# Mixer A's attention with keys on partitions: scores of three heads in one matmul, maxima from an extra pass

## The reference

```python
def gqa_attention(q, k, v):                # 6 query heads, 2 key heads, head width 64
    ...
    scale = Dh ** -0.5
    def block(qblk):                       # 128 queries
        s = jnp.einsum('bqngd,bsnd->bngqs', qblk, k) * scale
        p = jax.nn.softmax(s, axis=-1)
        return jnp.einsum('bngqs,bsnd->bqngd', p, v)
    ...
# latent queries: keys are the 1024 latent keys and 128 cached context keys
out_a = gqa_attention(qa, jnp.concatenate([ka, ck_a], axis=1), jnp.concatenate([va, cv_a], axis=1))
# prompt queries: keys are the 128 prompt keys
out_a = gqa_attention(qa, ka, va)
```

## Time and profile before

| | us |
|---|---|
| median of 3 runs | 3603.79 (3602.97 to 3606.46) |
| the profiled execution, device time | 3604.08 |
| its span, first to last instruction | 3602.3 |
| tensor engine busy in the span | 3340.2 |
| mixer A's attention, layer 0 | 175.70 to 368.54 |
| mixer A's attention, layer 1 | 1952.90 to 2145.04 |

### The profile page before, as it was taken

One profiled execution on the slowest core, in us unless ns is written; L12 is line 12 of the kernel. 1 busy time (PEld: TensorE's weight loads), 2 busy tenths in 40 slices (PEclk: granted clock), 3 DMA queues, 4 the chain that ended last, 5 costly groups with the idle time before them and its releaser, 6 DMA issues. The chain is left out here.

```text
span 3602.3 us, 48329 instructions
## 1 busy us (share of the span) xinstructions
PE 3340.2 (93%) x18844; PEld 2783.5 (77%) x18844; DVE 1319.7 (37%) x2333; ACT 1496.2 (42%) x2904; POOL 1396.1 (39%) x836
## 2 busy tenths in 40 slices
PE   6799999987999999999986999998979999999998
PEld 4478666776789989989964876676857899999997
DVE  2656333156641131131127643333565311311212
ACT  3255333124554454454423543331335544444443
POOL 1400011015765565565523000000167555655654
PEclk8899999998999999999987999999989999999999
DMA  5000121146544444444400001110535444444443
GB/s 197 12 8 1 43 65 30 42 156 201 177 129 127 143 134 129 144 133 156 146 28 20 1 25 43 43 41 31 195 100 175 129 124 146 145 125 146 147 125 115
DMA packets 310450, 367.41 MB, mean 102 GB/s; under 512 B 20160, under 2 KB 252880, under 8 KB 310224
## 3 DMA queue, kind: packets, MB, share of 16 engines
q1 hardware_dynamic: 310080, 364.19, 31.8%
q10 hardware_dynamic: 144, 0.13, 0.0%
HBM read 343.97 MB, written 20.30 MB: 101 GB/s over the span
## 5 line engine op out<-in xcount | busy, mean ns | idle before, releaser
L2070 POOL TENSOR_TENSOR w_lo<-w_raw,w_hi 128x1024 fp32r<-128x1024 f32 x432 | 1054.1, 2441 | 720.4 <-ACT w_hi L1991 720.0
L1991 ACT CAST w_hi<-w_raw 128x1024 fp32r<-128x1024 f32 x432 | 453.6, 1050 | 916.0 <-PE ps L1941 547.6
L2100 DVE TENSOR_TENSOR u_lo<-mix,u_hi 128x384 fp32r<-128x384 f32 x192 | 266.6, 1388 | 1212.7 <-ACT u_hi L2002 1212.7
L1939 PE MATMUL ps<-h_hi,w_hi 128*128 128x384 f32 x1536 | 517.6, 337 | 2.8 <-ACT mix L1998 2.8
L1941 PE MATMUL ps<-h_hi,w_lo 128*128 128x384 f32 x1536 | 516.4, 336 | 0.0
L1940 PE MATMUL ps<-h_lo,w_hi 128*128 128x384 f32 x1536 | 515.3, 335 | 0.0
L1958 PE MATMUL ps<-w_hi,u_lo 128*128 128x512 f32 x1152 | 453.2, 393 | 0.0
L1957 PE MATMUL ps<-w_lo,u_hi 128*128 128x512 f32 x1152 | 453.0, 393 | 0.0
L1956 PE MATMUL ps<-w_hi,u_hi 128*128 128x512 f32 x1152 | 450.9, 391 | 0.0
L1939 PEld LDWEIGHTS ps<-h_hi,w_hi 128*128 128x128 f32 x1536 | 289.3, 188 | 10.0 <-issue 3.2
L1940 PEld LDWEIGHTS ps<-h_lo,w_hi 128*128 128x128 f32 x1536 | 289.1, 188 | 6.8
(11 more groups left out here) (267 smaller groups left out, 4988.0 us busy)
## 6 DMA issues: line engine op xcount, KB each, us to landing
w_raw<-in_w_ffn_up SPq DMA_DIRECT2D x192, 512.0 KB, 4.1
w_raw<-in_w_ffn_down SPq DMA_DIRECT2D x192, 512.0 KB, 3.3
ring<-in_w_ada SPq DMA_DIRECT2D x80, 512.0 KB, 5.7
out_y_sample<-x SPq DMA_DIRECT2D x32, 512.0 KB, 2.9
w_raw<-in_w_out SPq DMA_DIRECT2D x30, 512.0 KB, 3.5
x<-out_y_sample SPq DMA_DIRECT2D x24, 512.0 KB, 5.0
ring<-in_w_in SPq DMA_DIRECT2D x18, 512.0 KB, 5.4
w_raw<-in_w_out SPq DMA_DIRECT2D x36, 256.0 KB, 4.2
```

The source lines that it names most:

```text
L1939: pe.matmul(ps[:, 6, 0:CW], wh[:, k, :], hi[:, k, cc], start=(k == 0), stop=False)
L1991: act.copy(w_hi[:, i % 3, :], raw[:, i % 3, :]).then_inc(sem("piece_hi"), 1)
L2070: pool.tensor_tensor(w_lo[:, i % 3, :], raw[:, i % 3, :], w_hi[:, i % 3, :].bitcast(F32), ALU.subtract).then_inc(sem("piece_lo"), 1)
L2100: dve.tensor_tensor(u_lo[:, j % 2, m, :], square[:, i % 2, :], u_hi[:, j % 2, m, :].bitcast(F32), ALU.subtract).then_inc(sem("m_u_lo"), 1)
```

## The change

`attention()` is gone and `turned_attention()` takes its place, with a stream for POOL too. Keys lie on the partitions of the scores and queries along the columns, for the three query heads of one key head at once: `scores_turned(i, g)` puts 3 x 128 queries against one key slot. The result needs no transposes to be applied to the values. A row's maximum and sum now run across partitions, and are made in other ways:

- One extra pass, `scores(x)`: the scores in the old layout, with KH alone (512 + 512 + 128 columns), only for `maximum(x)` on DVE. All 54 units go through the same three banks, 0 to 2.
- POOL's `make_diag(i)` multiplies six identity matrices by a tile's six columns of maxima. `shift(i)` on the tensor engine sums them over the partitions (weights `select`, ones on one half), which lays the negated maxima along the columns, in bank 0. ACT's `copy_shift(i)` copies them to the free half of `q2`; POOL's `copy_high(i)` puts the high query part on the other.
- The low-key pass takes `q2` in place of Q: KL's free half now holds 1/64 in place of zero (`clear_low(pool, KL, 1.0 / HD)`), so 64 rows of 1/64 times the shift add it to each score in the same matmul.
- `exp(i, g)` needs no bias: 128x384 from one of three PSUM banks (3 to 5) to one of six slots of a ring in the free part of `mix`.
- Sums: DVE (`add`, "first", "pair", "more", "part") and POOL (`add`, "pair", "more") add the probabilities of the nine slots up into `total`; `denominator(i)` sums it over the partitions with a matmul of ones (fp32, 64-column halves), in bank 0; `output(i)` takes the reciprocal of 128x384 and multiplies the output of three heads by it.
- The tensor engine's order: steps of three key slots, three steps a latent tile, one for the prompt tile, which now comes last. Two units of the extra pass go into each step, up to two tiles ahead. The applies of a step follow a step later.
- `bank_free()` guards bank 0 to 2 before each `scores`, `shift` and `denominator`.

The diff, cut to its core:

```diff
-            def clear_low(pool, k_low):
+            def clear_low(pool, k_low, value=0.0):
...
-            def attention(tag, units, own, n_keys):
...
+            def turned_attention(Q, KH, KL, V, own):
+                TILES = list(range(LAT)) + [PROMPT]
+                SLOTS = [list(range(LAT)) + [CTX_SLOT]] * LAT + [[PROMPT]]
+                W = 3 * P
+                RING = 6
...
+                steps = [(i, c) for i in range(nt) for c in range((len(SLOTS[i]) + 2) // 3)]
+                units = [(i, j, m) for i in range(nt) for j in range(2) for m in range(3)]
...
+                def turned_scores(b):
+                    return ps[:, 3 + b % 3, 0:W]
+                def out_of(i):
+                    return ps[:, 6 + i % 2, 0:W]
+                def upto(s):
+                    return min(6 + min(3 * (s + 1), 2 * (s + 1) + 2), len(units))
+                def sum_ops(i, c):          # (DVE's adds, POOL's adds)
+                    g = list(chunk(i, c))
+                    if len(SLOTS[i]) == 1:
+                        return [("first", (g[0],))], []
+                    if c == 0:
+                        return [("pair", (g[0], g[1])), ("more", (g[2],))], []
+                    if c == 1:
+                        return [("more", (g[0],))], [("pair", (g[1], g[2]))]
+                    return [("more", (g[0],)), ("more", (g[1],)), ("part", ())], [("more", (g[2],))]
...
+                def tensor(pe):
+                    def bank_free():
+                        pe.wait_ge(max_ready, taken["max"])
+                        if taken["shift"]:
+                            pe.wait_ge(shift_copied, 2 * taken["shift"])
+                        if taken["den"]:
+                            pe.wait_ge(den_taken, taken["den"])
+                    def scores(x):
+                        i, j, m = units[x]
+                        if x:
+                            bank_free()
+                        a = Q[:, j, m, columns(TILES[i])]
+                        runs = [(PROMPT, 1, 0)] if TILES[i] == PROMPT else [(0, 4, 0), (4, 4, 512), (CTX_SLOT, 1, 1024)]
+                        for slot, n, at in runs:
+                            mm = pe.matmul(psf[:, at:at + n * P], a, KH[:, j, slot * P:(slot + n) * P], start=True, stop=True)
+                        mm.then_inc(s1_ready, 1)
+                        taken["max"] += 1
+                    def shift(i):
+                        pe.wait_ge(diag_ready, i + 1)
+                        bank_free()
...
+                        for j in range(2):
+                            mm = pe.matmul(ps[:, 0, 0:W], select[:, j, :], diag[:, 3 * j:3 * j + 3, :].rearrange("p m n -> p (m n)"), start=(j == 0), stop=(j == 1))
...
+                    def scores_turned(i, g):
+                        kk, tt = columns(slot_of(i, g)), columns(TILES[i])
+                        if g == first[i]:
+                            pe.wait_ge(shift_copied, 2 * (i + 1))
+                            pe.wait_ge(high_copied, i + 1)
+                        for j in range(2):
+                            b = 2 * g + j
+                            if b >= 3:
+                                pe.wait_ge(exp_done, b - 2)
+                            at = turned_scores(b).rearrange("p (m n) -> p m n", m=3)
+                            pe.matmul(at, KH[:, j, kk], Q[:, j, :, tt], start=True, stop=False)
+                            pe.matmul(at, KL[:, j, kk], q2[:, i % 2, j, :, :], start=False, stop=True).then_inc(st_ready, 1)
+                    def apply(i, c):
...
+                        for g in chunk(i, c):
+                            pe.wait_ge(exp_done, 2 * g + 2)
+                            for j in range(2):
+                                mm = pe.matmul(out_of(i)[half(j), :], V[:, slot_of(i, g), half(j)], probs(g)[:, j, :],
+                                               start=(g == first[i]), stop=(g + 1 == first[i + 1]))
...
+                    def denominator(i):
+                        pe.wait_ge(summed, i + 1)
+                        bank_free()
+                        for j in range(2):
+                            mm = pe.matmul(ps[half(j), 0, 0:W], ones[:, half(j)], total[:, i % 2, j, :], start=True, stop=True)
...
+                    for x in range(6):
+                        scores(x)
+                    shift(0)
+                    x = 6
+                    for s, (i, c) in enumerate(steps):
+                        for g in chunk(i, c):
+                            scores_turned(i, g)
+                            if x < upto(s):
+                                scores(x)
+                                x += 1
+                        if i + 1 < nt and c == 2:
+                            shift(i + 1)
+                        if s >= 1:
+                            apply(*steps[s - 1])
+                        if i >= 1 and (c == 1 or i + 1 == nt):
+                            denominator(i - 1)
+                    apply(*steps[-1])
+                    denominator(nt - 1)
...
+                def gpsimd(pool):
+                    def make_diag(i):
+                        pool.wait_ge(max_ready, 6 * (i + 1))
...
+                        pool.tensor_tensor(diag[:, :, :], ident[:, :].unsqueeze(1).to_broadcast([P, 6, P]),
+                                           n.unsqueeze(2).to_broadcast([P, 6, P]), ALU.mult).then_inc(diag_ready, 1)
...
+                def vector(dve):
...
+                    def output(i):
+                        dve.wait_ge(den_ready, i + 1)
+                        dve.reciprocal(rden[:, :], ps[:, 0, 0:W]).then_inc(den_taken, 1)
+                        dve.wait_ge(den_taken, i + 1)
+                        dve.tensor_tensor(mix_turned[:, 0:3, columns(TILES[i])], out_of(i).rearrange("p (m n) -> p m n", m=3),
+                                          rden[:, :].rearrange("p (m n) -> p m n", m=3), ALU.mult).then_inc(out_done, 1)
+                    for x in range(6):
+                        maximum(x)
+                    x = 6
+                    for s, (i, c) in enumerate(steps):
+                        adds = [(steps[s - 1][0],) + a for a in sum_ops(*steps[s - 1])[0]] if s >= 1 else []
+                        late = [a for a in adds if a[1] == "part"]
+                        adds = [a for a in adds if a[1] != "part"]
+                        while x < upto(s):
+                            maximum(x)
+                            x += 1
+                            if adds:
+                                add(*adds.pop(0))
+                        for a in adds + late:
+                            add(*a)
+                        if i >= 1 and (c == 1 or i + 1 == nt):
+                            output(i - 1)
...
-                                clear_low(pool, KL)
+                                clear_low(pool, KL, 1.0 / HD)
...
-                    tensor, scalar, vector = attention("attn_a", units, own, 9 * P)
+                    tensor, scalar, gpsimd, vector = turned_attention(Q, KH, KL, V, own)
```

More of the change, by code:

```diff
@@ L519, in unit_operands @@
                 return (q[:, j], [(k[:, j, a:z], k_low[:, j, a:z], c) for a, z, c in segments])
-            def clear_low(pool, k_low):
+            def clear_low(pool, k_low, value=0.0):
                 for j in range(2):
-                    pool_step(pool.memset(k_low[half(1 - j), j].bitcast(F32), 0.0))
-            def attention(tag, units, own, n_keys):
[L533 to L570, removed]
-                def tensor(pe):
-                    def scores(i):
-                        if i >= 2:
[L576 to L649, removed]
-                        act.copy(rden_T[:, p % 2, :], rden_p(p)).then_inc(rden_copied, 1)
-                    exp(0)
-                    for i in range(nu):
-                        copy_groups(act, 0, i)
-                        if i + 1 < nu:
-                            exp(i + 1)
-                        if i % 2 == 1 and i >= 3:
-                            take_rden(i // 2 - 1)
-                    take_rden(nu // 2 - 1)
-                def vector(dve):
-                    def maximum(i):
-                        u = units[i]
-                        dve.wait_ge(S_ready, i + 1)
-                        dve.tensor_reduce(nmax[:, i % 4:i % 4 + 1], S(i, 0, u["n"]), AX.X, ALU.max, negate=True).then_inc(max_ready, 1)
-                    def spread_rden(p):
-                        s = 2 * p % 4
-                        dve.wait_ge(exp_done, 2 * p + 2)
-                        dve_step(dve.reciprocal(rden[:, s:s + 2], den[:, s:s + 2]))
-                        if p >= 2:
-                            dve.wait_ge(rden_turned, p - 1)
-                        dve.tensor_copy(spread[:, p % 2, :, :], rden[:, s:s + 2].unsqueeze(2).to_broadcast([P, 2, HD])).then_inc(rden_spread, 1)
-                    def output(p):
-                        dve.wait_ge(rden_copied, p + 1)
```

(15 more changed lines are left out.)

140 lines of the change are left out of this document (129 added, 11 removed).

## The result

The changed kernel takes 3652.21 us (median of 4 runs, 3646.97 to 3654.20), the kernel before 3603.38 on the same chip: ratio 1.0135, 95% interval 1.0117 to 1.0152. It is slower, as forecast, by 49 us where 68 were predicted. The profiled execution took 3651.58 us, 47.5 above that of before.

The account below looks back on a forecast made before the run. Tensor instructions were taken to bound the stage before; the change adds waits on shared score banks. Profiled 3604.1 + 2 layers x 27.7 + 13 for the clock = 3672 us; own range 3640 to 3705, 8 in 10 for 3630 to 3712.

Parts of the forecast that it names:

- start: Start of each attention stage: six score passes at 1.2 GHz, diagonal, shift, copies; first turned scores at 22.1 us.
- tile 0: First latent tile: doubled slots and three score passes in each of its first two steps; 21 plus 8.0, 29.2 us.
- tiles 1 to 5: Five latent tiles of each layer at 23.9 us each, five waits (6.5 us) in each: 119.6 us.
- tile 6: Latent tile whose last step has the prompt's 128-column units: 6.5 + 7.1 + 7.6 = 21.2 us.
- tile 7: Tile with nearly no score passes: ACT paces turned scores to 2.6 a step, last step awaits the reciprocal; 15.8 us.
- end: End of each stage: two reciprocals in a row, the last adds and the prompt's denominators between; 12.3 us.
- The steps of a tile: Three steps of a latent tile: waits of 1.08 us behind maxima, 2.21 behind the reciprocal; 23.9 us, 1.9 more than before.
- Applies: Applies of 384 columns: halves overlap at 0.161 us each; rival without overlap adds some 95 us, 3767, chance 0.06.
- The rival in which the waits are covered: Five waits of each tile covered, only tensor work counts: faster, about 3568 us with no waits; chance 0.08.
- The rival with the low clock throughout: Clock stays at 1.2 GHz through the attention stage: tiles of about 36.6 us, 3812 us in all; chance 0.03.
- Adds beside POOL: DVE adds slowed by POOL: 1.3 us each before a maximum, up to 16 us as an unknown; cost taken as 0.
- The clock in the tiles: Clock falls after the reciprocal's wait: 0 or some 2.2 us a tile, 0 to 26 in all; half, 13, taken.

Follow-up runs that it names:

- Experiment 7: Changed kernel with denominators copied out early, division moved later, two bank sets for the first six passes, and reordered tensor and DVE queues: 3577.03 us, 0.9923 of the kernel before.
- experiment 1: Changed kernel with DVE copying the denominators out of PSUM and taking the reciprocal from that copy at once: 3671.87 us, ratio 1.0192 to the kernel before.
- experiment 5: Changed kernel with the second score pass of the first two steps of tiles 1 to 7 behind the third slot of turned scores: 3646.48 us, ratio 1.0114.
- experiment 10: The later second score pass on the changed kernel, plus 24 unread matmuls of 128 columns ahead of the pass waiting for the reciprocal: 3646.43 us, ratio 1.0112.

## Why the prediction was right, step by step

The direction and its cause were right: by difference, 22.06 - 17.7 = 4.4 us of tensor work and other time left a tile, 5.8 us of waits came, and DVE was busy for 70% of it (16.54 of 23.60), as forecast. The terms, in us per layer (boundaries are the first turned scores of a tile):

| term | predicted | layer 0 | layer 1 |
|---|---|---|---|
| start | 22.1 | 20.26 | 20.25 |
| tile 0 | 29.2 | 23.96 | 24.24 |
| tiles 1 to 5 | 119.6 | 121.83 | 118.63 |
| tile 6 | 21.2 | 20.89 | 22.25 |
| tile 7 | 15.8 | 15.36 | 15.36 |
| end | 12.3 | 12.75 | 12.07 |
| sum | 220.2 | 215.05 | 212.80 |

- **The steps of a tile.** Predicted 6.49, 7.13 and 10.28; measured 6.52, 7.16 and 9.91 at the full clock. Waits: 6.5 predicted, 5.8 by taking them away (3.81 and 1.98). The hand-over from the end of a maximum to the next pass was 0.05 us, not 0.15; from the end of the reciprocal it was 0.15. The waits came out 0.7 shorter and the work between them 0.3 longer than predicted, so that the tile as a whole, 23.56 against 23.9, is closer than its parts: that much was luck.
- **The reciprocal.** 2.55 from 6.25 ns a column; measured 2.557.
- **Applies.** Twelve in 2.16 us with the tail of the last. The two halves of a pair start within 0.01 us of each other and the next pair 0.32 later, 0.16 an apply: the halves overlap at 384 columns, and that rival falls.
- **The rival in which the waits are covered.** Its tile, less waits, was about right: 17.7, by difference, against 17.4. Its condition, waits under 3.0 us, didn't hold here. Experiment 7 meets it, by order in the tiles, and then the kernel is faster.
- **The rival with the low clock throughout** falls: the granted clock was 0.90 and 0.92 over the two stages.
- **Adds beside POOL.** The mean add took 0.99 against 0.95 alone: 2.7 us in the run, of the 16 allowed.
- **Tile 0, mis-sized by 5.2 and 5.0.** What failed is that the clock stays low for its first two steps, 21 us. It was up 5 us after the first turned scores in layer 0 (slots of 0.18 from 200.78 on, 0.32 before) and 6 us after in layer 1; the two steps took 16.1 and 16.4.
- **The start, mis-sized by 1.8 a layer.** Units came every 2.78 us, not 3.0.
- **The clock in the tiles, 13 predicted.** The windows of tiles 1 to 5 at 23.56 each would give 117.8; the rest is 4.0 in layer 0 and 0.8 in layer 1, and tile 6 of layer 1 has 1.4 more than that of layer 0: 6.2. The price in one tile, 0.8 to 2.3, kept to the bound of about 2.2, but fewer tiles had one. The 13 was half of a bound, a guess, and its ground was weak: the prediction set its two gaps apart by little work around the first, but the trace has the tensor engine busy for 7.49 of the 10.1 us that end with it (411.00 to 421.10), as much as for the 75% around the other.
- **Left out of the sum:** 4.6 us outside the stages, 1.7 of them the projections' lower clock; the rest is within the spread there.

Together: 68.4 predicted for the stages and the clock, 42.9 measured. Of the 25.5 between them tile 0 is 10.2, the clock 6.8, the start 3.7, tiles 1 to 5 at full clock 3.6 and the rest 1.2. With the 4.6 outside the stages, which the forecast did not have and which lie the other way, the profiled time came out 20.9 us below the forecast.

## What to carry to other kernels

When a change takes tensor work out but makes two steps share one buffer, write down the time from one user of that buffer to the next (matmul, hand-over, reader's own time, and all that stands ahead of the reader in its queue) and count what the queue can do meanwhile; here the 2.15 us from pass to pass had the pass's own 0.54 and one slot of 0.75 in them. Freeing the buffer early did nothing while the next reader stood behind the same long instruction on its engine (experiment 1); that one belongs behind what others wait for. The order of the queues, with the early copy and a second set of banks for the first six passes (11 us in the stages), turned 49 us of loss into 26 us of gain.

## What the hardware showed that was not expected

- A wait of 1.9 us, once a tile, lowered the granted clock of the work behind it in nine of ten tiles of experiment 5, at up to 2.2 us a tile; matmuls whose results nobody reads, put into that wait, made the kernel 16.2 us faster.
- Matmuls of 128 columns in a row (24 in 2.79 us, 14 in 1.67) take 0.11 us each by their starts. Only the first, behind one of 384 columns, takes 0.06. Rows 3 have both: 0.06 for the first of two behind 512 columns (231.06 to 231.12), 0.12 for the second (to 231.24). The expectation of experiment 10 priced all 24 at 0.06.
- The reciprocal costs the same from SBUF (2.553 us) as from PSUM (2.557).
